# Triangular inverse of the second mixer's prompt half: 16x16 blocks by substitution on VectorE, two tiles in buffers of their own

## What is computed

```python
# second mixer (gated delta rule), per chunk and head
b = jnp.cumsum(gc, axis=-1)
dec = jnp.exp(jnp.where(incl, b[..., :, None] - b[..., None, :], -jnp.inf))
kb = kc * bc[..., None]
L = jnp.where(strict, jnp.einsum('bhtd,bhsd->bhts', kb, kc) * dec, 0.0)
rhs = jnp.concatenate([vc * bc[..., None], kb * jnp.exp(b)[..., None]], axis=-1)
X = lax.linalg.triangular_solve(L, rhs, left_side=True, lower=True, unit_diagonal=True)
...
# first mixer (gated linear attention): state of every sample sequence
o = jnp.einsum('bhtd,bhdv->bhtv', qc * jnp.exp(b), S) + jnp.einsum('bhts,bhsv->bhtv', A, vc)
S = jnp.exp(b_last[:, :, 0, :, None]) * S + jnp.einsum('bhsd,bhsv->bhdv', kc * jnp.exp(b_last - b), vc)
```

## Time and profile before

| | us |
|---|---|
| median of 3 runs | 916.95 |
| lowest and highest run | 912.99, 917.04 |
| profiled execution, its own time | 913.24 |
| its span | 911.3 |
| PE busy in the span | 825.8 (91%) |
| DVE busy | 404.8 (44%) |
| ACT busy | 251.2 (28%) |
| POOL busy | 57.0 (6%) |
| stretch from step 29 to the sample output of the first mixer | 59.00 |
| stretch from step 37 to step 59 | 202.12 |

### The profile page before, as it was taken

One profiled execution on the slowest core, in us unless ns is written; L12 is line 12 of the kernel. 1 busy time (PEld: TensorE's weight loads), 2 busy tenths in 40 slices (PEclk: granted clock), 3 DMA queues, 4 the chain that ended last, 5 costly groups with the idle time before them and its releaser, 6 DMA issues.

```text
span 911.3 us, 12572 instructions
## 1 busy us (share of the span) xinstructions
PE 825.8 (91%) x4822; PEld 566.7 (62%) x4822; DVE 404.8 (44%) x1074; ACT 251.2 (28%) x617; POOL 57.0 (6%) x131
## 2 busy tenths in 40 slices
PE   4899998998999899999999999998499999999984
PEld 2566666776666688878887778786334443444422
DVE  1310024756556864575557268622323343333413
ACT  2211122846137233333333323421011101110112
POOL 4000000104000100020000030000000000000001
PEclk9999999989689999999999999997599999999997
DMA  9968876213276311123113565899879999999971
GB/s 271 387 210 290 298 253 209 87 58 102 93 222 194 93 47 47 47 85 94 47 47 98 158 173 157 260 334 397 327 268 391 395 397 392 394 398 393 391 278 53
DMA packets 115011, 201.25 MB, mean 221 GB/s; under 512 B 3364, under 2 KB 61111, under 8 KB 114903
## 3 DMA queue, kind: packets, MB, share of 16 engines
q1 hardware_dynamic: 111156, 191.28, 60.2%
q0 software_dynamic: 3088, 7.38, 2.6%
q10 hardware_dynamic: 710, 1.79, 0.5%
HBM read 187.85 MB, written 12.13 MB: 219 GB/s over the span
## 4 chain that ended last, share of the span: by engine, by line
PE 68%; DVE 10%; DMA 7%; SPq 6%; ACT 4%; issue 3%; POOL 1%; DVEq 0%; POOLq 0%; ACTq 0%
PE bank L649 26%; PE bank L1070 13%; SPq L2462 5%; PE bank L477 4%; PE bank L978 3%; DMA arena<-in_w_exp_down 3%; PE bank L818 3%; PE bank L590 2%; PE bank L808 2%; PE bank L824 2%; PE bank L1115 2%; DVE arena L1340 2%; PE bank L718 1%; PE bank L929 1%; DMA arena<-in_x_sample 1%
## 5 line engine op out<-in xcount | busy, mean ns | idle before, releaser
L649 PE MATMUL bank<-arena 128*128 128x288 f32 x1152 | 307.0, 422 | 2.7 <-DVE arena L1225 1.4
L649 PEld LDWEIGHTS bank<-arena 128*128 128x128 f32 x1152 | 221.4, 197 | 72.8 <-issue 12.2
L1070 PE MATMUL bank<-arena 128*64 128x512 f32 x768 | 173.1, 603 | 9.2 <-DVE arena L1856 7.7
L1070 PEld LDWEIGHTS bank<-arena 128*64 128x64 f32 x768 | 56.4, 138 | 107.5 <-issue 105.3
L477 PE MATMUL bank<-arena 128*128 128x128 f32 (+5 forms) x388 | 61.7, 292 | 31.7 <-DMA arena<-h_rows,arena 10.8
L477 PEld LDWEIGHTS bank<-arena 128*128 128x128 f32 (+5 forms) x388 | 44.6, 144 | 59.9 <-issue 25.6
L2062 ACT ACTIVATE arena<-arena 128x288 f32<-128x288 f32 (+1 forms) x56 | 25.0, 448 | 150.6 <-DVE arena L1325 150.6
L1864 DVE SCALAR_TENSOR_TENSOR arena<-bank,arena 128x256 f32<-128x256 f32 x64 | 30.5, 476 | 27.4 <-PE bank L1115 27.4
L1340 DVE SCALAR_TENSOR_TENSOR arena<-arena 128x312 f32<-128x312 f32 x72 | 39.2, 544 | 2.5
L1841 DVE SCALAR_TENSOR_TENSOR arena<-bank,arena 128x512 f32<-128x512 f32 x8 | 5.5, 692 | 69.6 <-ACT arena L2239 69.6
L1957 ACT ACTIVATE arena<-arena 128x288 f32<-128x288 f32 (+4 forms) x60 | 33.0, 550 | 2.0
(11 more groups left out here) (345 smaller groups left out, 963.6 us busy)
## 6 DMA issues: line engine op xcount, KB each, us to landing
arena<-in_w_in SPq DMA_DIRECT2D x36, 1024.0 KB, 6.0
arena<-in_w_exp_gate SPq DMA_DIRECT2D x8, 4096.0 KB, 25.6
arena<-in_w_exp_up SPq DMA_DIRECT2D x8, 4096.0 KB, 27.8
arena<-in_w_exp_down SPq DMA_DIRECT2D x8, 4096.0 KB, 28.5
arena<-in_w_ada SPq DMA_DIRECT2D x24, 1024.0 KB, 9.7
arena<-in_state_gla SPq DMA_DIRECT2D x4, 1024.0 KB, 5.3
out_gla_s<-arena SPq DMA_DIRECT2D x4, 1024.0 KB, 8.2
out_gdn_s<-arena SPq DMA_DIRECT2D x4, 1024.0 KB, 8.5
```

Of the source, the lines that this page charges most:

```text
L649: last = mm(b[:, 0:TOK], w[:, k, 128 * j:128 * j + 128], hT[:, k, :], k == 0, k == KD - 1)
L1070: last = mm(out[SLOTS * x:SLOTS * x + SLOTS, :], lhs[:, k, SLOTS * x:SLOTS * x + SLOTS], wt[:, k, 512 * half:512 * half + 512], k == 0, k ...
```

## The change

The sizes: `BLOCK = 16`, `FIRST_LEVEL = 4`. Levels 0 to 3 of the two prompt tiles are replaced. ACT writes the eight 16x16 diagonal blocks of LT to DRAM (`low_rows`, one DMA for each block row, all heads), POOL reads them back as 64 rows, one for each block and head, of 256 elements (`lowB`). DVE inverts all 64 in 15 columns, each an outer product and a subtraction that wait for each other by semaphore. ACT writes the result to DRAM (`inv_rows`), POOL reads it back as 128 rows (`invC`), and DVE spreads it to block-diagonal X (`gdn_spread`), from where levels 4 to 6 go on as they were; level 6 takes only the quarter of the product that is not zero.

Tile 1 gets E, AT and LT of its own, in the room of buffers that are free by then (`GB`, and `SA` once the first mixer's state is stored, which is why that store is now behind step 28, ahead of the placements). The name `ke` for LT is gone. The table `GDN_PROMPT_AT` now has a step for each piece and tile. The gates stand a step ahead of the scores. The states of the first mixer stand a step later and wait for the placements ahead of the read; the state products take turns between the two sequences.

```diff
-GLA_STATES_AT = (29, 30, 31, 32)
-GDN_PROMPT_AT = (38, 48)
+GLA_STATES_AT = (30, 31, 32, 33)
+GDN_PROMPT_AT = {"gdn_gates": (37, 39), "gdn_scores": (38, 40), "gdn_blocks": (40, 41), "gdn_inverse0": (42, 45),
+                 "gdn_inverse1": (43, 46), "gdn_back": (44, 47), "gdn_spread": (47, 53), "gdn_level4": (47, 53),
+                 "gdn_level5": (48, 54), "gdn_level6": (49, 55), "gdn_values": (50, 56), "gdn_out": (51, 57),
+                 "gdn_turn": (52, 58)}
...
+    Es = (E, carve(HB, P, at=GB_at), E)
+    ATs = (AT, carve(HB, P, at=GB_at + HB * P), AT)
+    LTs = (LT, carve(HB, P, at=SA_at), LT)
...
 def gla_states(c):                                   # PE
+            def update(g):
+                two = [take(5 + 2 * g, f"gla state {2 * c} {g}"),
+                       ring_bank(f"gla states {c}") if g else take(6, f"gla state {2 * c + 1} {g}")]
+                for hh in range(2):
+                    h = 2 * g + hh
+                    for x in range(2):
+                        s_ = 2 * c + x
+                        rows = slice(32 * (s_ % 4), 32 * (s_ % 4) + DT)
+                        last = mm(two[x][:, 256 * hh:256 * hh + 256], keaP[rows, s_ // 4, 128 * h:128 * h + 128],
+                                  vaP[rows, s_ // 4, 256 * h:256 * h + 256])
...
             pe.wait_ge(*when("gla keys placed"))
             pe.wait_ge(*when("gla values placed"))
+            read()
+            update(0)
+            update(1)
...
 def gdn_level(m, lv):                                # PE
+                    if lv == LEVELS - 1:
+                        last = mm(b[64:128, 64 * j:64 * j + 64], Lm[0:64, h, 64:128], X[0:64, h, 1, 0:64])
+                        continue
...
+        def gdn_inverse(m, half):                    # DVE
+            low, inv = lowB[m], invB[m][:, :, 1]
+            if not half:
+                dve.wait_ge(*when(t + "blocks in"))
+                dve.wait_ge(*when(t + "blocks cleared"))
+            for c in (range(0, 8), range(8, BLOCK - 1))[half]:
+                rows, cols = BLOCK - 1 - c, c + 1
...
+                if c:
+                    dve.wait_ge(*when(t + f"column {c - 1}"))
+                V.tensor_tensor(o, low[:, c, c + 1:BLOCK].unsqueeze(2).to_broadcast(shape),
+                                inv[:, c, 0:cols].unsqueeze(1).to_broadcast(shape), ALU.mult) \
+                    .then_inc(mark("gdn_inverse", t + f"outer {c}"), 1)
+                dve.wait_ge(*when(t + f"outer {c}"))
+                V.tensor_tensor(left, left, o, ALU.subtract) \
+                    .then_inc(mark("gdn_inverse", t + f"column {c}"), 1)
...
+        def gdn_spread(m):                           # DVE
+            dve.wait_ge(*when(t + "inverse in"))
...
+            for g in range(2):
+                for o in range(2):
+                    src = invC[:, 4 * g:4 * g + 4, o, :].unsqueeze(2).to_broadcast(shape)
+                    V.tensor_tensor(X[:, 4 * g:4 * g + 4, o, :].rearrange("p h (d s) -> p h d s", s=BLOCK), src, mask,
+                                    ALU.mult) \
...
+            block_matrix(m, FIRST_LEVEL)
...
+        def gdn_blocks(m):                           # ACT
+            for d in range(P // BLOCK):
+                rows = slice(BLOCK * d, BLOCK * d + BLOCK)
+                act.dma_start(low_rows[m, d].rearrange("h s t -> s h t"), LTs[m][rows, :, rows]) \
...
+        def gdn_back(m):                             # ACT
+            act.wait_ge(*when(t + "inverted"))
+            for d in range(P // BLOCK):
+                act.dma_start(inv_rows[m, d].rearrange("t h o s -> h t o s"), invB[m][HB * d:HB * d + HB]) \
...
+        def gla_stored(m):                           # POOL, behind step 28
+            if m:
+                pool.wait_ge(*when("gla state prompt 1"))
+                pool.dma_start(O["gla_p"].rearrange("h k v -> k h v"), SA) \
...
+        def gdn_blocks(m):                           # POOL
+            pool.wait_ge(*when(t + "blocks out"))
+            for p in (38, 39):
+                pool.wait_ge(*when(f"tap3 {p}"))
...
+            pool.dma_start(lowB[m].rearrange("p s t -> p (s t)"), low_rows[m].rearrange("d h s t -> (d h) (s t)")) \
```

More of the change, by code:

```diff
@@ L258, in _program @@
     Lm = carve(HB, P)
+    Y_at = top[0]
     Y = carve(HB, P)
@@ L388, in _program @@
         stand(at, "gla_states", c)
-    for m, first in enumerate(GDN_PROMPT_AT):
-        stand(first, "gdn_scores", m)
-        for lv in range(LEVELS):
-            stand(first + 1 + lv, "gdn_level", m, lv)
-        for i, part in enumerate(("gdn_values", "gdn_out", "gdn_turn")):
-            stand(first + 1 + LEVELS + i, part, m)
+    for part, steps in GDN_PROMPT_AT.items():
+        for m, at in enumerate(steps):
+            if part[-1].isdigit():
+                stand(at, part[:-1], m, int(part[-1]))
+            else:
+                stand(at, part, m)
     for part, at, *lv in GDN_SAMPLE_AT:
@@ L702, in gla_states @@
             w = slot(("sgla", c)).rearrange("p (s h) v -> p s h v", h=HA)
-            b = take(4, t + "oS") if c == 0 else pm[4]
-            for s_ in (2 * c, 2 * c + 1):
-                for h in range(HA):
-                    last = mm(b[32 * h:32 * h + 32, 0:DVA], qbM[:, h, 32 * s_:32 * s_ + 32], w[:, s_ % 2, h, :],
-                              s_ == 0, s_ == NSEQ - 1)
-            last.then_inc(mark("gla_products", f"gla states read {c}", *([t + "oS ready"] if c == 3 else [])), 1)
+            def update(g):
[8 more added lines that the diff above has]
+                                  vaP[rows, s_ // 4, 256 * h:256 * h + 256])
+                        if hh:
+                            last.then_inc(mark("gla_products", f"gla state product {s_} {g}"), 1)
@@ L709, in gla_states, with read @@
+            def read():
+                b = take(4, t + "oS") if c == 0 else pm[4]
+                for s_ in (2 * c, 2 * c + 1):
+                    for h in range(HA):
+                        last = mm(b[32 * h:32 * h + 32, 0:DVA], qbM[:, h, 32 * s_:32 * s_ + 32], w[:, s_ % 2, h, :],
+                                  s_ == 0, s_ == NSEQ - 1)
+                last.then_inc(mark("gla_products", f"gla states read {c}", *([t + "oS ready"] if c == 3 else [])), 1)
             pe.wait_ge(*when("gla keys placed"))
@@ L803, in gdn_level @@
                 pe.wait_ge(*when(t + f"Lm{lv} {g}"))
+                if lv == FIRST_LEVEL and m < 2:
+                    pe.wait_ge(*when(t + f"X{lv - 1} {g}"))
                 b = take(4 + g, t + f"Y{lv} {g}")
@@ L1427, in gla_states @@
                                                       ALU.mult, ALU.add)
-                    last.then_inc(mark("gla_by_vector", f"gla state {s_} {g}"), 1)
+                    last.then_inc(mark("gla_by_vector", f"gla state {s_} {g}",
+                                       *([f"read gla states {c}"] if g and x else [])), 1)
         def gla_out(m):
@@ L1586, in gdn_values @@
                 hs = slice(HG * g, HG * g + HG)
+                if m == 0:
+                    dve.wait_ge(*when("gdn1 inverse out"))
                 dve.wait_ge(*when(t + f"y{g}"))
```

147 lines of the change are left out of this document (98 added, 49 removed).

## The result

The changed kernel takes 864.48 us (median of 4 runs, 859.64 to 868.77) against 915.81 (four runs of the kernel before; the 916.95 above is the median of the first three): a ratio of 0.9442, 95% interval 0.9384 to 0.950. Faster, as forecast (859, range 843 to 883). The profiled execution took 859.64 (span 857.8) against 913.24 (911.3), so 53.6 less; the forecast for it was 56.

A forecast was written before the change was run, and what follows sets the result against it. The prediction took PE to bound the kernel (68% of the chain of waits), DVE next (10%). Savings of 14 + 40 + 2 = 56 from 913.24 gave 857 for the profiled execution; half of 3.7 added made 859, range 843 to 883.

The forecast's parts named there:

- What bounds the kernel: Whole program: chain of waits on PE for 68% of the span; what the mixers save carries over one to one.
- Part A: First mixer's sample states, a step later with alternating products: 260.4 to 265.5 against 276.99, 14 saved (8 to 17).
- the products: First mixer's states: products alternating between two sequences take 1.7 a state instead of 3.16 or 3.22.
- Part B: Second mixer's triangular inverse, steps 37 to 59: 69.2 to first level 4 plus 92.8 after, against 202.1; 40 saved.
- the wait for the blocks: DVE before tile 0's substitution waits 4 for diagonal blocks through DRAM, there at 37.1, blocks landing at 41.1.
- The substitution: DVE's inversion of the diagonal blocks: 60 small dependent operations at 0.265 each, 15.9 (bounds 12.6 and 32).
- PE's half: Second mixer from first level 4 to step 59: PE leads, 92.8 including 1.8 for the clock after waits.
- Part C: Second mixer's updates: the same alternation of products between sequences saves 2 (0 to 3).
- Rival 1: Triangular inverse: DVE is hidden and PE stays the bound, saving 51, time 848; chance 0.13.
- Rival 2: Triangular inverse: trips through DRAM are slow, landings 8.3 instead of 3.7, +16, time 875; chance 0.18.
- Rival 3: First mixer's states keep the low clock or placements land later: part A gives 4, not 14, 869; chance 0.12.
- Rival 4: Substitution on DVE: dependent small operations cost 0.5 each, +16, time 875; chance 0.06.

The follow-up runs named there:

- last run: Changed kernel with tile 1's substitution and inverse issues later, 140 semaphore instructions added on PE, and POOL issuing the inverse stores: 857.63 us, ratio 0.9363.

## Why the prediction was right, point by point

- **What bounds the kernel.** Right: what PE lost in the mixers came off the end one to one; from step 71 to the last weights the two traces are 0.9 apart.
- **Part A**, forecast 14 (8 to 17), measured 13.7. The wait (3.17 for 3.2) and its cause are right, and so is the arrival of PE. That the sum came out is in part luck: the dip behind the wait cost 3.4 (0.7 and 2.7) for 1.8 and the products 1.2 more than forecast, and the 2.6 that were held back for dips at the later states were not needed, as none came. The step that failed is the one on the products: "the products now alternate between two sequences", so "I take the products at 1.7". They took 2.00, and two runs show that taking turns gave 0.1 a state and the fourth bank 1.1, and the dips besides. The earlier trace rows were read rightly for the second mixer and carried over to a place where a bank, not the array, set the pace: the row of 3.22 in the earlier trace rows shows no idle time, since it is a group of 16 passes, and the late start of its last four passes lies inside it.
- **Part B**, forecast 40, measured 41.2, from 69.2 + 92.8 foreseen and 65.5 + 95.4 found. (The terms of the 69.2 add up to 69.5, those of the blocks' 41.1 to 40.9; neither slip matters.) Of the 69.2, the wait for the blocks (4) and 2.0 of substitution did not come; DVE's work of the steps beside and behind it took some 2 more than the estimate for it.
  - The substitution: 30 operations and a copy from 312.17 to 321.5 with one step between; 3.72 for the first 16 and 3.24 for the other 14, so 0.232 each, 13.9 for 60 where 15.9 was forecast. The row of 0.25 was the right one to take.
  - The wait for the blocks, forecast 4, was none: the blocks landed at 312.08, 37.05 after the start of step 37, DVE was there at 37.1 as forecast. The step that failed is the landing, "3.7 to land" taken from the earlier trace rows; ACT's small stores landed 1.6 after the last issue began (305.47 to 307.09), ACT began 1.6 sooner, and the load took 4.7, beside a weight load (307.25 to 312.97). The view of DMA issues of the changed kernel, KB each and median us from issue to landing:

```profile
low_rows<-arena ACTq DMA_DIRECT2D x16, 8.0 KB, 1.6
...
arena<-inv_rows POOLq DMA_DIRECT2D x2, 128.0 KB, 2.4
arena<-low_rows POOLq DMA_DIRECT2D x2, 64.0 KB, 5.0
```

  - The inverse's way back was just hidden, as forecast: inverted at 321.5, back at 334.99, the spread at 337.39. It was not quick: ACT began 2.7 late, and its stores landed 5.4 after the last issue began, beside a weight load (326.10 to 331.74).
  - PE's half: 95.4 for 92.8. "Hold its activations of steps 41 and 44 ... I cost them at nothing (uncovered, 4.2 each)" is the step that failed. It named steps 41 and 44, and the costly one was tile 1's, at step 47, ahead of a copy that PE waits for: 2.37, and 1.8 of clock, for which the forecast had set aside its 1.8. Two runs put the two together at 4.1, near the uncovered price, though nearly half of it is clock and not issues.
- **Part C**, forecast 2 (0 to 3), measured 0. Its bound counted PE and DVE; the limit was SP's order, the load behind a store.
- **Rival 1** (DVE hidden) fell: what was added to DVE came through to level 4, 7.1 of 7.2, and PE waited some 5 in all ahead of level 4. It was near, though: 9 was forecast for that wait. **Rival 2** fell: no landing took the 8.3 of the bound. The Trainium skill, "DMA: Bandwidth & Descriptors", Specifications, has transfers below 512 bytes read, modified and written; no price of that shows here, where stores in runs of 64 bytes landed in 1.6 and stores in runs of 128 bytes, with no weight load beside them, in 2.1 to 2.3. **Rival 3** fell: the stage's granted clock was 0.93 for 0.81, and its placements landed as forecast. **Rival 4** fell with 0.20 to 0.25 a step. In a sentence apart: the Trainium skill, "VectorE: DVE Perf Modes", "The TRN2 errata", gives besides its table a formula for an fp32 tensor_tensor add with a fixed term of 151 cycles, by which 15 and 64 elements would take 0.173 and 0.224; the trace agrees with 0.168 and 0.223, and not with the table's 0.08 and 0.13.
- **Not foreseen**: 4.4 at the end, from where PE's code stands but for 0.3 of POOL's DRAIN (the runs with the code moved give 4.1 and 4.4 of it back), and 2.3 less at the start, where step 25 to step 26 took 9.66 in the profiled execution (11.35 to 12.62 in all others). The second takes back half of the first in the profiled execution, which is the fastest of its four; the median, without that luck, is 5.5 above the forecast.

## What to carry to other kernels

A group of passes with no idle time ahead of it can still hold a wait inside: where a group takes longer than its passes end to end, look at the single starts and at who last read the bank. An engine that issues DMAs is busy for each issue, so a store that nobody waits for belongs behind the copy that somebody waits for. How soon a small transfer lands depends on what moves beside it: look for a large load in the same microseconds before blaming its size. Work moved from PE to a chain of small operations on DVE pays as long as PE has other work of that length beside it; here 8 us of the chain taken out of PE's way gave 2.5, since PE was then full again.

## What the runs showed of the hardware

- **A taken branch and where the code stands.** PE's one branch, past the overflow code, took 3.38 to 3.72 in all runs with PE's code about as long as the changed kernel's and 0.36 to 0.39 where 140 instructions, or the longer code of before, moved it; 16 KB of code were loaded at 839.25, as PE stood there. The Trainium skill, "Runtime: NRT & Kernel Launch", "Instruction fetch mechanics", says that code is fetched in sequence, in blocks of 256 instructions, and that a branch out of what is held waits for its target's block; the runs agree. A change that takes some 650 instructions from PE can so lose some 4 us at the far end of the program, and gain them back with instructions that do nothing.
- **The clock.** A stop in each state's products (0.48 from one pass to the next, 0.21 is usual), with no other idle time, went with a fall of the granted clock from 2.4 to 1.2 GHz in the projection behind it (mean 0.71 of full), 5.84 for 4.15; without the stop there was none. Dips of 1.7 also come and go between executions in the same code (step 59 to step 66 took 51.55 or 53.24), so two profiles are best compared stretch by stretch.
- **Issuing.** Stores of 128 runs cost ACT 0.28 to 0.48 for each issue, in single cases 1.06 and 1.68, and POOL 0.6. Each DMA that POOL issued made its DRAIN at the end of the program some 0.08 longer (6.70, 7.03 and 8.33 with 57, 61 and 77).
- **Landing beside a large load.** POOL's loads of 64 KB from DRAM took 4.4 to 5.3 in the changed kernel and all its variants, each beside a weight load of 1 MB; its loads of 128 KB took 2.2 to 2.5 with none beside them, and 3.7 in the one case that overlapped one (366.24 to 369.92, last run).
